# All norms of a two-layer decoder trunk turned unscaled, with the token factor applied where products are read

## The chip, the core and the metric

The kernel runs on one core of a Trainium2 chip. Its metric is the device time of one execution in microseconds. Before the change three runs took 1270.37 to 1271.36 us, with a median of 1271.24. The profile is of a further execution.

A core has TensorE (PE) for matrix products into eight banks of PSUM, VectorE (DVE), ScalarE (ACT) and GpSimd (POOL) for elementwise work, and SyncE (SP), which here only issues transfers. Each engine works through its own instructions in order and waits on semaphores.

## What is computed

A stream x of 256 tokens by 1024 features passes two layers, then a last RMS norm. The reference, cut to what matters:

```python
def rmsnorm(x, w):
    y = x * lax.rsqrt(jnp.mean(x * x, axis=-1, keepdims=True) + NORM_EPS)
    return y * w

memn = rmsnorm(mem, mem_norm_w)
for layer in range(2):
    x = x + 0.5 * swiglu(rmsnorm(x, norm_w[layer, 0]), w_gate[layer, 0], w_up[layer, 0], w_down[layer, 0])
    h = rmsnorm(x, norm_w[layer, 1])
    x = x + (even_mixer(h, ...) if layer % 2 == 0 else odd_mixer(h, ...))
    x = x + cross_attention(rmsnorm(x, norm_w[layer, 2]), memn, wq[layer], wkv[layer], wo[layer])
    x = x + 0.5 * swiglu(rmsnorm(x, norm_w[layer, 3]), w_gate[layer, 1], w_up[layer, 1], w_down[layer, 1])
return rmsnorm(x, final_norm_w)
```

`swiglu(h)` is `(silu(h @ w_gate) * (h @ w_up)) @ w_down` with 2816 hidden features. The even mixer projects h to retention heads (q, k rotated, v, a gate), and to a state-space part: x, B and C go through a causal convolution of four taps and a silu, a step size dt through a softplus with logarithms, and decays between tokens are sums of dt. The odd mixer is sparse and sliding-window attention. The cross attention has four heads over 256 memory tokens, whose keys and values come from `memn`.

A norm has two factors: a weight per feature, and a factor per token, 1/rms (`rstd`). The token factor commutes with a projection: (rstd * x * w) @ W = rstd * ((x * w) @ W).

## The kernel before

**Weights.** All weight matrices stream once through a ring of three slots, in chunks of 1 MB (128 partitions x 2048 floats), on SyncE's queue. `chunk_plan` fixes their order. Each float is split in two parts of lower precision: ScalarE copies `raw` to `w_hi` (`hi_upto`, 1.9 us), VectorE subtracts to `w_lo` (`lo_upto`, 2.3 us), and TensorE adds hi*hi, hi*lo and lo*hi: 48 products of 128x256 or their equal, 5.8 us in a projection and 5.6 in a feed-forward stage. SyncE issues the next load of a slot when VectorE has split it (`lo_done`). `hi_upto(n)` and `lo_upto(n)` make all chunks below n that are not made yet; where such a call stands among other work is written out by hand, engine by engine.

**Stages.** Each layer: a feed-forward stage of 11 turns (gate, up, down chunk), the mixer, the cross attention, a second feed-forward stage. Norms are numbered v: 0 and 5 before the first feed-forward of each layer, 2 and 6 before the mixers, 3 and 7 before the crosses, 4 and 8 before the second feed-forwards, 9 at the end, 1 for the memory.

**Norms.** A projection needs x feature by token (`hT_hi`, `hT_lo`), so TensorE transposes x: 16 transposes of 128x128, as four blocks (t, kh), t for the tokens and kh for half of the features. There are two ways. In the *rows way* (v = 1, 2, 3, 6, 7, 9) ScalarE squares x (`squares`, L614), GpSimd makes `rstd` (L1526, L1528), VectorE scales x to `xn` (`norm_rows`, L1060), TensorE transposes `xn` (L1675), and ScalarE and VectorE split the result from PSUM (`evac_hi` L623, `evac_lo` L1080). In the *column way* (v = 0, 4, 5, 8) TensorE transposes raw x, the weight is applied in the split (`weighted_hi` L632, `weighted_lo` L1070), the squares go beside it, and the token factor is spread over the partitions as a row by a small product (L1769) and applied to gate and up results in the feed-forward stage (L725, L1125). Norm 5 also has two of its blocks transposed between the products of the last down chunk (`turn_ahead`). The memory's norm goes the rows way in the first feed-forward stage, and TensorE transposes it ahead of that stage's last down chunk (`mem_turned`).

**Fillers.** The eight chunks of keys and values of each layer need only the memory. TensorE runs them where it would wait (`FILL` at the norms, `kv_chunk` within the mixers). Chunk (0, 0), the first keys, stands in the even mixer.

**Even mixer.** ScalarE reads each bank of the three convolution chunks x0 to x2 to a padded buffer (L801) and makes the first tap with the bias (L806), VectorE adds six products for the other taps (L1248). ScalarE makes the silus and, for dt, exponentials and logarithms with two table loads. Then VectorE rotates q and k out of PSUM (L1235, four times), GpSimd combines (L1547, L1548) and makes weights for the decay sums (L1572, twice eight), for which TensorE waits at L1935.

## Time and profile before

| | |
|---|---|
| median of three runs | 1271.24 us |
| the profiled execution | 1270.32 us, its span 1268.5 us |
| TensorE products busy | 1243.3 us, 98% |
| VectorE, ScalarE, GpSimd busy | 760.7 us (60%), 624.5 us (49%), 77.5 us (6%) |
| share of the chain that ended last | TensorE 92%, GpSimd 2%, VectorE 2%, ScalarE 2% |
| moved by DMA | 215.29 MB, 170 GB/s in the mean, 284 GB/s in the first of 40 slices |
| mean granted clock of TensorE | 0.990 of full speed |

Idle time of an engine other than TensorE costs nothing by itself. The page gives each group of instructions its busy time and what ended the idle time ahead of it. A single row of the timeline is a run of equal instructions: its start, its length, the engine, the line in the kernel, the operation, output and input tiles, and how many; in brackets the wait ahead of it and the instruction that ended it.

### The profile page before, as it was taken

The numbers are of one execution on the slowest core, as the hardware profiler recorded it, in microseconds if no ns is written. First come the engines' busy times: TensorE is split into PE (matmuls) and PEld (weight loads), VectorE is DVE, ScalarE is ACT, GpSimd is POOL, SyncE is SP. The second block draws the span as 40 slices with busy tenths as digits, with TensorE's granted clock in tenths as the row PEclk, the third lists the DMA queues.
The fourth block names the chain that finished last, engine by engine and source line by source line (L and its number), as shares of the span: only waits on it lengthen the run. The fifth ranks groups of instructions, "written<-read, shape, count | busy, mean of one in ns | idle before, by whom it ended". The sixth has DMA issues, their size and how long they took to land.

```text
span 1268.5 us, 18583 instructions
## 1 busy us (share of the span) xinstructions
PE 1243.3 (98%) x7546; PEld 1098.7 (87%) x7546; DVE 760.7 (60%) x760; ACT 624.5 (49%) x816; POOL 77.5 (6%) x99
## 2 busy tenths in 40 slices
PE   8999998999999999999999999999999999999997
PEld 7888887999989888888898888899877898888886
DVE  6666666754654576665676656645565545756655
ACT  6454445653435464444464444444565345644442
POOL 1000000450110010000010000010000100100000
PEclk9999999999999999999999999999899999999999
DMA  8766663544353455565555655555421434655551
GB/s 284 266 214 199 184 197 117 170 148 148 134 182 133 133 188 187 188 198 183 180 178 188 198 187 179 182 164 180 154 100 34 149 134 133 199 184 181 197 192 40
DMA packets 176931, 215.29 MB, mean 170 GB/s; under 512 B 14768, under 2 KB 159344, under 8 KB 176880
## 3 DMA queue, kind: packets, MB, share of 16 engines
q1 hardware_dynamic: 175792, 211.32, 52.0%
q0 software_dynamic: 864, 3.15, 0.7%
q8 instruction: 37, 0.61, 0.2%
q10 hardware_dynamic: 224, 0.10, 0.0%
q14 instruction: 14, 0.11, 0.0%
HBM read 213.50 MB, written 1.05 MB: 169 GB/s over the span
## 4 chain that ended last, share of the span: by engine, by line
PE 92%; POOL 2%; DVE 2%; ACT 2%; issue 1%; DMA 1%; SPq 0%; DVEq 0%; POOLq 0%; ACTq 0%
PE ps L1620 25%; PE ps L1599 15%; PE ps L1600 15%; PE ps L1601 15%; PE ps L1635 13%; PE ps L1861 1%; PE ps L1675 1%; PE ps L1839 1%; PE ps L2152 1%; POOL xk L1572 1%; ACT w_hi L601 1%; PE ps L2168 1%; ACT ps L614 1%; DVE w_lo L1044 1%; POOL arena L1547 1%
## 5 line engine op out<-in xcount | busy, mean ns | idle before, releaser
L1620 PE MATMUL ps<-hT,w_hi 128*128 128x512 f32 x1392 | 333.3, 392 | 2.2 <-DVE hT L1070 2.2
L1620 PEld LDWEIGHTS ps<-hT,w_hi 128*128 128x128 f32 x1392 | 259.1, 189 | 55.1 <-DVE hT L1070 2.4
L1150 DVE TENSOR_TENSOR w_lo<-raw,w_hi 128x2048 fp32r<-128x2048 f32 x108 | 247.6, 2292 | 62.2 <-ACT w_hi L707 62.2
L1044 DVE TENSOR_TENSOR w_lo<-raw,w_hi 128x2048 fp32r<-128x2048 f32 (+1 forms) x93 | 203.6, 2199 | 125.7 <-ACT w_hi L601 125.5
L707 ACT ACTIVATE w_hi<-raw 128x2048 fp32r<-128x2048 f32 x108 | 206.0, 1908 | 0.0
L601 ACT ACTIVATE w_hi<-raw 128x2048 fp32r<-128x2048 f32 (+1 forms) x92 | 167.8, 1839 | 50.6 <-PE ps L1601 47.1
L1635 PEld LDWEIGHTS ps<-hT,w_lo 128*128 128x128 f32 x1408 | 180.5, 191 | 6.8
L1635 PE MATMUL ps<-hT,w_lo 128*128 128x256 f32 x1408 | 182.6, 283 | 0.0
L1599 PE MATMUL ps<-w_hi,arena_r 128*128 128x512 f32 (+1 forms) x384 | 148.7, 387 | 0.0
L1600 PE MATMUL ps<-w_lo,arena_r 128*128 128x512 f32 (+1 forms) x384 | 148.1, 386 | 0.0
L1601 PE MATMUL ps<-w_hi,arena_r 128*128 128x512 f32 (+1 forms) x384 | 147.8, 385 | 0.0
L1599 PE MATMUL ps<-w_hi,hT 128*128 128x256 f32 (+2 forms) x352 | 113.9, 323 | 0.0
L1600 PE MATMUL ps<-w_lo,hT 128*128 128x256 f32 (+2 forms) x352 | 112.9, 321 | 0.0
L1601 PE MATMUL ps<-w_hi,hT 128*128 128x256 f32 (+2 forms) x352 | 112.9, 321 | 0.0
L1526 POOL TENSOR_SCALAR msq<-msum 128x1 f32<-128x1 f32 x20 | 22.0, 1100 | 1072.2 <-ACT ps L614 659.2
L699 ACT ACTIVATE arena_r<-arena 128x512 fp32r<-128x512 f32 x44 | 27.8, 631 | 119.0 <-PE ps L1601 112.8
L1601 PEld LDWEIGHTS ps<-w_hi,arena_r 128*128 128x128 f32 x384 | 72.1, 188 | 16.1
L680 ACT ACTIVATE arena<-ps 128x512 f32<-128x512 f32 x44 | 26.4, 600 | 118.2 <-PE ps L1635 118.2
L1599 PEld LDWEIGHTS ps<-w_hi,arena_r 128*128 128x128 f32 x384 | 72.3, 188 | 13.9
L1600 PEld LDWEIGHTS ps<-w_lo,arena_r 128*128 128x128 f32 x384 | 72.1, 188 | 13.8
L694 ACT ACTIVATE arena<-ps 128x512 f32<-128x512 f32 x44 | 26.4, 600 | 100.3 <-PE ps L1635 100.3
L1599 PE MATMUL ps<-hT,w_hi 128*128 128x256 f32 x264 | 75.7, 287 | 0.0
(266 smaller groups left out, 1753.5 us busy)
## 6 DMA issues: line engine op xcount, KB each, us to landing
raw<-in_ffn_w_up SPq DMA_DIRECT2D x44, 1024.0 KB, 5.3
raw<-in_ffn_w_down SPq DMA_DIRECT2D x44, 1024.0 KB, 4.8
raw<-in_ffn_w_gate SPq DMA_DIRECT2D x43, 1024.0 KB, 5.3
raw<-in_xattn_wkv SPq DMA_DIRECT2D x16, 1024.0 KB, 5.4
raw<-in_even_w_in SPq DMA_DIRECT2D x13, 1024.0 KB, 5.2
raw<-in_xattn_wq SPq DMA_DIRECT2D x8, 1024.0 KB, 5.1
raw<-in_xattn_wo SPq DMA_DIRECT2D x8, 1024.0 KB, 5.7
raw<-in_even_w_out SPq DMA_DIRECT2D x4, 1024.0 KB, 4.9
```

What stands on the lines that cost most here:

```text
L601: ins = nc.scalar.activation(hi, src, ACT.Copy)
L680: nc.scalar.activation(gate_lo, ps[:, 0:2, SEQ:], ACT.Copy).then_inc(gate_copied, 1)
L694: nc.scalar.activation(up_lo, ps[:, 2:4, SEQ:], ACT.Copy).then_inc(up_copied, 1)
L699: nc.scalar.activation(dst, gu.rearrange("p (k c) -> p k c", k=2), ACT.Copy).then_inc(gu_hi_done, 1)
L707: nc.scalar.activation(w_hi[:, m % RING, :], raw[:, m % RING, :], ACT.Copy).then_inc(hi_done, 1)
L1044: ins = V.tensor_tensor(lo, src, hi.bitcast(F32), ALU.subtract)
L1150: V.tensor_tensor(w_lo[:, m % RING, :], raw[:, m % RING, :], w_hi[:, m % RING, :].bitcast(F32), ALU.subtract).then_inc(lo_done, 1)
L1599: mm(dst, l_hi, r_hi, start=start, stop=False)
L1600: mm(dst, l_hi, r_lo, start=False, stop=False)
L1601: return mm(dst, l_lo, r_hi, start=False, stop=stop)
L1620: mm(ps[:, bank0 + m, :], cols(w_hi, n, k, CW, m * P, (m + 1) * P), hT[:, k, :, :].rearrange("p a c -> p (a c)"), start=k == 0, stop=False)
L1635: last = mm(ps[:, bank0 + m, SEQ:], cols(w_lo, n, k, CW, m * P, (m + 1) * P), hT[:, k, 0, :], start=False, stop=k == KT - 1)
```

## The change

- All norms but the last go the column way, with two blocks transposed inside the last chunk before them (`turn_ahead` before norms 2, 3, 5, 6 and 7). `norm_rows` is left for the last norm alone, and its weight row is loaded late.
- Mixers and crosses take the token factor where their products are read. TensorE spreads it as a row behind the first projection (`rstd_rows`), ScalarE copies the row, and VectorE multiplies with it the results that lie feature by token: the conv chunks (L1270), the queries of the crosses (L1225) and of the odd mixer. These reads were ScalarE's. Results that lie token by feature get it as a scale per partition: on ScalarE in two ACTIVATEs (`tokens_out`), in the rotation on VectorE as a third operand.
- x and the memory are also handed in feature by token (`xT`, `memT`, 1 MB each) and loaded to `turned_raw`. Norm 0 and the memory's norm have no transposes any more: ScalarE and VectorE split `turned_raw` with the weight (`turned_hi`, `turned_lo`), for the memory in turn 7 of the first feed-forward stage. The memory's token factor goes on the keys (VectorE, `k_out`) and values (ScalarE).
- x by token is loaded behind up chunk 0, and ScalarE squares it behind its copy of up chunk 1.
- The key chunk (0, 0) is the filler of norm 2 and has a buffer of its own.
- 13 instead of 10 first products of no use (`WARM`).

```diff
-            take(kv[:7])
+            take(kv[1:7])
...
+        FILL = {("norm", 0, 1): (0, 0), ("norm", 0, 2): (0, 7), ...
...
                 if first:
                     for kh in range(2):
                         ks = slice(4 * kh, 4 * kh + 4)
+                        sp.dma_start(turned_raw[:, ks, :], d["xT"][:, ks, :]).then_inc(xT_in[kh], 16)
                         sp.dma_start(slot_k(base, CW)[:, ks, :], gate[0][:, ks, :])\
...
                 load(base + 1, slot_k(base + 1, CW), up[0])
+                if first:
+                    for t in range(TT):
+                        sp.dma_start(x[:, t, :], d["x"][0, t * P:(t + 1) * P, :]).then_inc(x_in[t], 16)
...
                 hi_upto(base + 4)
-                act.wait_ge(row_mm, f + 1)
-                nc.scalar.activation(rstd_row[:, :], ps[:, 5, 0:SEQ], ACT.Copy).then_inc(row_read, 1)
+                if f == 0:
+                    squares(0, x, lambda t, h: act.wait_ge(x_in[t], 16))
+                row_copy(norm_no(layer, 3 * which), 5)
...
             def even():
                 E = at["even", "x0"]
+                row_copy(2, 7)
                 for c in range(3):
-                    act.wait_ge(chunks_used, E + c + 1)
-                    if c == 0:
-                        act.wait_ge(es["xpad_zero"], 1)
-                    nc.scalar.activation(ev.xpad[:, 2 * c:2 * c + 2, CONV_W - 1:],
-                                         ps[:, c, :].rearrange("p (a c) -> p a c", a=2),
-                                         ACT.Copy)
+                    act.wait_ge(es["xpad_done"], c + 1)
                     for m in range(2):
                         k = 2 * c + m
-                        ins = nc.scalar.activation(ev.xbcT[:, k, :], ps[:, c, m * SEQ:(m + 1) * SEQ], ACT.Identity,
+                        ins = nc.scalar.activation(ev.xbcT[:, k, :], ev.xpad[:, k, CONV_W - 1:], ACT.Identity,
...
+            def k_out(layer, i):
+                dve.wait_ge(chunks_used, at["kv", layer, i] + 1)
+                dve.wait_ge(mem_row_done, 1)
+                V.tensor_tensor(keys(layer, i),
+                                ps[:, KV_BANK[layer][i], :].rearrange("p (a c) -> p a c", a=2),
+                                mem_row[:, :].unsqueeze(1).to_broadcast([P, 2, MEM]), ALU.mult).then_inc(k_read, 1)
...
+                    V.tensor_tensor(ev.xpad[:, 2 * c:2 * c + 2, CONV_W - 1:],
+                                    ps[:, c, :].rearrange("p (a c) -> p a c", a=2),
+                                    rstd_row.unsqueeze(1).to_broadcast([P, 2, SEQ]), ALU.mult)\
+                     .then_inc(es["xpad_done"], 1)
...
+            def rstd_rows(v, bank):
+                pe.wait_ge(rstd_done, 2 * v + 2)
+                rows_of(rstd, bank).then_inc(row_mm, 1)
...
                     turn(j, False)
-                if f == 0:
-                    mem_turned()
...
-                if f == 1:
-                    hidden_down((f + 1) * FJ, n, False, True, turn_ahead(5, ("norm", 1, 0)))
+                if f < 3:
+                    key = ("norm", layer + which, 1 - which)
+                    hidden_down((f + 1) * FJ, n, False, True, turn_ahead(norm_no(key[1], key[2]), key))
...
-                out_chunks(at["mixout", 0, 0], last_bank=lambda: pe.wait_ge(kv_read, 7))
+                out_chunks(at["mixout", 0, 0], last_bank=lambda: pe.wait_ge(*kv_out(0, 6)),
+                           between=turn_ahead(3, ("norm", 0, 2)))
```

ScalarE in the first feed-forward stage, before (the first row is the second half of gate chunk 0, the `w_hi` rows below the squares are up 0, gate 1 and, with `chunks_used`, up 1; the last row copies the factor's row):

```order
L651 ACTIVATE w_hi<-raw 128x1024 [waits raw_in0]
L614 ACTIVATE xn,msum<-x 128x512 [waits x_in0] x2
L614 ACTIVATE xn,msum<-x 128x512 [waits x_in1] x2
L601 ACTIVATE w_hi<-raw 128x2048 [waits raw_in1]
L601 ACTIVATE w_hi<-raw 128x2048 [waits raw_in2]
L680 ACTIVATE arena<-ps 128x512 [waits chunks_used]
L601 ACTIVATE w_hi<-raw 128x2048 [waits chunks_used,raw_in0]
L725 ACTIVATE arena<-ps 128x256 [waits row_mm]
```

And after, with the squares on the lines L627:

```order
L662 ACTIVATE w_hi<-raw 128x1024 [waits raw_in0]
L617 ACTIVATE w_hi<-raw 128x2048 [waits raw_in1]
L617 ACTIVATE w_hi<-raw 128x2048 [waits raw_in2]
L700 ACTIVATE arena<-ps 128x512 [waits chunks_used]
L617 ACTIVATE w_hi<-raw 128x2048 [waits chunks_used,raw_in0]
L627 ACTIVATE arena,msum<-x 128x512 [waits x_in0] x2
L627 ACTIVATE arena,msum<-x 128x512 [waits x_in1] x2
L668 ACTIVATE arena<-ps 128x256 [waits row_mm]
```

The four squares moved from ahead of up 0's copy to behind up 1's, right ahead of the copy of the row for which the factor is needed.

VectorE at the entry of the even mixer, before (`w_lo` rows split weight chunks, L1248 are taps):

```order
L1080 TENSOR_TENSOR hT<-ps,hT 128x4x128 [waits hT_hi_done] x4
L1044 TENSOR_TENSOR w_lo<-raw,w_hi 128x2048 [waits hi_done] x2
L1242 COPY arena<-ps 8x256 [waits e_dt_mm]
L1248 SCALAR_TENSOR_TENSOR arena<-arena,conv_w 128x256 [waits e_act_read]
L1248 SCALAR_TENSOR_TENSOR arena<-arena,conv_w 128x256
L1248 SCALAR_TENSOR_TENSOR arena<-arena,conv_w 128x256 [waits dve_step]
L1248 SCALAR_TENSOR_TENSOR arena<-arena,conv_w 128x256
L1248 SCALAR_TENSOR_TENSOR arena<-arena,conv_w 128x256 [waits dve_step]
L1248 SCALAR_TENSOR_TENSOR arena<-arena,conv_w 128x256
L1044 TENSOR_TENSOR w_lo<-raw,w_hi 128x2048 [waits hi_done]
```

And after (L1088 reads the first keys, L1270 a conv bank, L1278 are taps):

```order
L1045 TENSOR_TENSOR w_lo<-raw,w_hi 128x2048 [waits hi_done]
L1088 TENSOR_TENSOR first_keys<-ps,mem_row 128x512 [waits mem_row_done,chunks_used]
L1045 TENSOR_TENSOR w_lo<-raw,w_hi 128x2048 [waits hi_done] x2
L1265 COPY arena<-ps 8x256 [waits e_dt_mm]
L1270 TENSOR_TENSOR arena<-ps,arena 128x2x256 [waits chunks_used,e_xpad_zero,row_read]
L1278 SCALAR_TENSOR_TENSOR arena<-arena,conv_w 128x256 [waits e_act_read]
L1278 SCALAR_TENSOR_TENSOR arena<-arena,conv_w 128x256
L1278 SCALAR_TENSOR_TENSOR arena<-arena,conv_w 128x256 [waits dve_step]
L1278 SCALAR_TENSOR_TENSOR arena<-arena,conv_w 128x256
L1278 SCALAR_TENSOR_TENSOR arena<-arena,conv_w 128x256 [waits dve_step]
L1278 SCALAR_TENSOR_TENSOR arena<-arena,conv_w 128x256
L1045 TENSOR_TENSOR w_lo<-raw,w_hi 128x2048 [waits hi_done]
```

The read of a conv bank now stands on VectorE ahead of the taps, behind ScalarE's copy of the row, and ScalarE's first tap (`e_act_read`) comes between that read and the other taps.

VectorE at norm 3, before (L1060 scales x, L1080 splits turned x, the `w_lo` rows are key/value chunk 7 and the first query weights):

```order
L1105 SCALAR_TENSOR_TENSOR x<-ps,x 128x512 [waits chunks_used]
L1060 SCALAR_TENSOR_TENSOR xn<-x,rstd,norm_w_rows 128x512 [waits rstd_done,norm_w_in]
L1060 SCALAR_TENSOR_TENSOR xn<-x,rstd,norm_w_rows 128x512
L1044 TENSOR_TENSOR w_lo<-raw,w_hi 128x2048 [waits hi_done]
L1060 SCALAR_TENSOR_TENSOR xn<-x,rstd,norm_w_rows 128x512 [waits rstd_done]
L1060 SCALAR_TENSOR_TENSOR xn<-x,rstd,norm_w_rows 128x512
L1080 TENSOR_TENSOR hT<-ps,hT 128x4x128 [waits hT_hi_done] x4
L1044 TENSOR_TENSOR w_lo<-raw,w_hi 128x2048 [waits hi_done] x4
```

And after (L1066 splits turned x, L1225 reads queries):

```order
L1118 SCALAR_TENSOR_TENSOR x<-ps,x 128x512 [waits chunks_used]
L1066 SCALAR_TENSOR_TENSOR hT<-ps,norm_cols,hT 128x128 [waits cols_hi_done]
L1066 SCALAR_TENSOR_TENSOR hT<-ps,norm_cols,hT 128x128 x3
L1066 SCALAR_TENSOR_TENSOR hT<-ps,norm_cols,hT 128x128 [waits cols_hi_done]
L1066 SCALAR_TENSOR_TENSOR hT<-ps,norm_cols,hT 128x128 x3
L1066 SCALAR_TENSOR_TENSOR hT<-ps,norm_cols,hT 128x128 [waits cols_hi_done]
L1066 SCALAR_TENSOR_TENSOR hT<-ps,norm_cols,hT 128x128 x3
L1045 TENSOR_TENSOR w_lo<-raw,w_hi 128x2048 [waits hi_done] x3
L1225 SCALAR_TENSOR_TENSOR arena<-ps,arena 128x512 [waits chunks_used,row_read]
```

The scaling of x is gone, and all splits of turned x stand ahead of the weight splits, of which one stood between them before.

## Rows read from the trace of the kernel before

**Rows 1.** Waits of TensorE: line <- releaser: total us, times, longest us
```profile
PE ps L1675 <- DVE xn L1060: 7.9, 4, 3.5
PE ps L1620 <- DVE hT L1070: 2.2, 1, 2.2
PE ps L1935 <- POOL xk L1572: 1.2, 1, 1.2
```

**Rows 2.** Timeline of the start: start us, us, engine line op out<-in xcount
```profile
8.12 0.69 DVE L1478 CAST w_hi<-raw 128x1024 fp32r<-128x1024 f32 x1 [8.12 <-DMA raw<-in_ffn_w_gate]
...
12.48 0.75 ACT L614 ACTIVATE xn<-x 128x512 f32<-128x512 f32 x1
...
14.84 0.31 ACT L614 ACTIVATION_READ_ACCUMULATOR xn<-x 128x1 f32 x1
...
16.45 0.57 POOL L1528 TENSOR_TENSOR rstd<-msq,neg_half 128x1 f32<-128x1 f32 x1
...
20.51 1.92 ACT L601 ACTIVATE w_hi<-raw 128x2048 fp32r<-128x2048 f32 x1 [1.27 <-DMA raw<-in_ffn_w_up]
...
21.40 0.68 DVE L1120 TENSOR_TENSOR arena<-arena,ps 128x512 f32<-128x512 f32 x1
...
24.12 3.92 PE L1620 MATMUL ps<-hT,w_hi 128*128 128x512 f32 x16
```

**Rows 3.** Windows of the start; the last three columns: TensorE's clock, DMA share, GB/s
```profile
2.00:4.00 2.00, 2.00 (x11) 2.00 (x11) 0.00 (x0) 1.04 (x1) 0.00 (x0) 1.00 0.84 286
...
12.00:14.00 2.00, 2.00 (x6) 1.51 (x6) 2.00 (x5) 2.00 (x6) 0.00 (x0) 0.50 1.10 348
```

**Rows 4.** Windows at norms 3 and 7
```profile
375.00:380.00 5.00, 4.88 (x27) 4.64 (x28) 3.11 (x6) 1.19 (x2) 0.65 (x1) 0.66 0.85 305
...
1005.00:1010.00 5.00, 2.92 (x24) 2.44 (x23) 4.24 (x5) 1.40 (x3) 3.10 (x3) 1.00 0.23 71
```

**Rows 5.** Timeline, memory's transposes and the entry of norm 2
```profile
191.25 1.91 PE L1675 MATMUL ps<-consts,xn 128*128 128x128 f32 x16
...
198.36 0.40 PE L1601 MATMUL ps<-w_hi,arena_r 128*128 128x512 f32 x1
...
207.39 0.38 PE L1599 MATMUL ps<-hT,small_w_hi 128*128 128x256 f32 x1 [1.41 <-DVE hT L1080]
```

**Rows 6.** Timeline at norm 5
```profile
634.17 0.61 PE L1675 MATMUL ps<-consts,x 128*128 128x128 f32 x4
...
639.31 1.13 DVE L1070 SCALAR_TENSOR_TENSOR hT<-ps,norm_cols,hT 128x128 fp32r<-128x128 f32 x4 [2.12 <-ACT hT L632]
...
640.36 2.29 DVE L1044 TENSOR_TENSOR w_lo<-raw,w_hi 128x2048 fp32r<-128x2048 f32 x1
...
640.80 3.82 PE L1620 MATMUL ps<-hT,w_hi 128*128 128x512 f32 x16
```

**Rows 7.** Timeline of the even mixer
```profile
216.76 1.01 ACT L806 ACTIVATE arena<-ps,conv_b,conv_w 128x256 f32<-128x256 f32 x2
...
217.81 2.71 DVE L1248 SCALAR_TENSOR_TENSOR arena<-arena,conv_w 128x256 f32<-128x256 f32 x6 [5.75 <-ACT arena L806]
...
220.44 2.29 DVE L1044 TENSOR_TENSOR w_lo<-raw,w_hi 128x2048 fp32r<-128x2048 f32 x1
...
238.62 2.44 POOL L1547 TENSOR_TENSOR arena<-arena 128x128 f32<-128x128 f32 x1 [32.86 <-DVE arena L1235]
```

**Rows 8.** Timeline at norms 3 and 7, TensorE
```profile
369.12 0.28 PE L1599 MATMUL ps<-w_hi,memT_hi 128*128 128x256 f32 x1
...
375.11 1.32 PE L1675 MATMUL ps<-consts,xn 128*128 128x128 f32 x8 [2.09 <-DVE xn L1060]
...
380.63 0.28 PE L1599 MATMUL ps<-hT,w_hi 128*128 128x256 f32 x1
...
1003.00 0.28 PE L1599 MATMUL ps<-w_hi,memT_hi 128*128 128x256 f32 x1
...
1013.02 0.28 PE L1599 MATMUL ps<-hT,w_hi 128*128 128x256 f32 x1
```

More of the change, by code:

```diff
@@ L452, in build @@
             pT = part(4096, [XH, 2, SEQ])
-            small = part(6144, [32])
+            small = part(6400, [32])
             nmax = small[:, 0:8]
@@ new lines, in row_copy, with norm @@
+            def row_copy(v, bank):
+                act.wait_ge(row_mm, nth(v) + 1)
+                nc.scalar.activation(rstd_row, ps[:, bank, 0:SEQ], ACT.Copy).then_inc(row_read, 1)
+            def norm(layer, i):
+                v = norm_no(layer, i)
+                weighted_hi(v, SETS["norm", layer, i])
+                squares(v, x, lambda t, h: act.wait_ge(x_added, 4 * (v - 2) + 2 * t + h + 1))
+                if v == 2:
+                    act.wait_ge(mem_row_mm, 1)
+                    nc.scalar.activation(mem_row[:, :], ps[:, 5, 0:MEM], ACT.Copy).then_inc(mem_row_done, 1)
@@ L880, in even, with tokens_out @@
                 kv_chunk(0, 6)
+            def tokens_out(dst, bank, func):
+                for t in range(TT):
+                    ins = nc.scalar.activation(dst[:, t, :], ps[:, bank, t * CW:(t + 1) * CW], func,
+                                               scale=rstd[:, t:t + 1])
+                ins.then_inc(es["act_read"], 1)
             def conv_silu(c):
@@ L1017, in _ @@
             norm(1, 1)
-            hi_upto(at["odd", ODD_ORDER[0]] + 3)
             odd()
-            hi_upto(at["wq", 1, 0])
-            norm(1, 2, ahead=at["wq", 1, 0] + 1)
+            hi_upto(at["wq", 1, 0] + 1)
+            norm(1, 2)
             cross(1)
@@ L1167, in ffn @@
                 lo_upto(base + 4)
-                dve.wait_ge(row_read, f + 1)
+                dve.wait_ge(row_read, nth(norm_no(layer, 3 * which)) + 1)
                 gate_scale(0)
@@ L1364, in odd @@
                         compress_in()
+                lo_upto(at["cmp", 0] + 4)
+                read("qs1", 0)
+                lo_upto(at["odd", "qs1"] + 4)
+                lo_upto(at["cmp", 1] + 4)
+                read("a", 3)
                 lo_upto(at["cmp", 3] + 3)
@@ L1489, in _ @@
             ffn(1, 0)
-            norm(1, 1)
+            lo_upto(at["odd", ODD_ORDER[0]] + 1)
+            k_out(1, 2)
             lo_upto(at["odd", ODD_ORDER[0]] + 3)
             odd()
-            norm(1, 2, ahead=at["wq", 1, 0] + 1)
             lo_upto(at["wq", 1, 0] + 3)
@@ L1667, in used, with transposes @@
                 return ins.then_inc(chunks_used, 1)
-            def transposes(w, ready, src=xn, blocks=None):
-                for t, kh in blocks or block_order(w):
+            def transposes(w, ready, src=xn, blocks=BLOCKS):
+                for t, kh in blocks:
                     ready(t, kh)
@@ L1765, in ffn @@
                 used(wide_lo(base + 1, 2))
[L1767 to L1771 removed]
+                rstd_rows(v, 5)
                 def turn(j, first):
```

468 lines of the change are left out of this document (240 added, 228 removed).

## The prediction

> **What bounds the kernel now.** I read the page first: TensorE is busy 1243.3 of 1268.5 us, and the chain that ended last is TensorE for 92% (both in the table above). So time is won only where TensorE does less, or stands less. Then TensorE's waits by releaser [rows 1]: four waits of its transposes for the scaled x of VectorE (7.9 us together), one for the split of turned x at the start (2.2) and one for GpSimd's segment weights in the even mixer (1.2) are those that the change touches. Last the timeline around each of them, and windows for the granted clock. TensorE's idle time is 25 us in all, 2% of the span; what decides is which of these few microseconds come back elsewhere. The matmuls of the three split products are untouched, and the 16 transposes of each later norm stay, so each part below is a sum over places. 0.2% of the time, about 2.5 us, is what a measurement of this kernel can tell from no change.
>
> **The start.** Before, gate chunk 1 starts at 24.12 [rows 2], right behind the small product that spreads the token factor over the partitions. That product was never late: the last square ended at 15.15 and GpSimd had the factor at 17.02, 1.9 after the squares. In the new order ScalarE squares x behind its copy of up chunk 1, and TensorE keeps the product ahead of gate 1. So gate 1 now hangs on the transfer of up 1. Ahead of that in the queue: x by feature and gate 0 (2 MB), up 0, x by token, gate 1; with up 1 it is 6 MB, 6.3 million bytes. Once it runs, the queue moves 348 GB/s and a little more (I take 355); in its first 2 us it moved 286 [rows 3]. The first half of gate 0, behind 1.57 million bytes in all, released VectorE at 8.12: 2 + 1.57 million / 355 GB/s = 6.4, and 1.7 until it was seen. By the same sum up 1 is seen at 2 + 17.7 + 1.5 = 21.2 (its issue waits for the split of gate 0 at about 13, when the queue is still full, so it isn't late by that). Copy 1.9, four squares 2.7 (12.48 to 15.15), GpSimd 1.9, the product 0.4 [all rows 2]: gate 1 starts at about 27.9, against 24.12. **+3.7.** The first matmul comes earlier, at about 7.8 for 10.94, since no transposes and no split behind them stand ahead; that only makes TensorE ready for gate 1 at about 20.6, and longer waiting. Bounds: +2.5, if the small loads beside the queue take nothing and up 1 is seen 1.2 earlier; +7.5, if 6.3 million bytes go at the rate of the first window.
>
> The clock: after TensorE's wait of 2.09 at 375.11 [rows 8] the granted clock was 0.66 over 5 us [rows 4], so 5 x 0.34 = 1.7 us of matmul time lost. After the wait of the same length in the window from 1005 it stayed at 1.00 (same rows). A wait of 7 us is worse than either; I take the fall. **+1.7.** The Trainium skill ("TensorE: Matmul & The Clock Gate", Part 1) says that an idle TensorE falls to half its 2.4 GHz, and that the moment at which the chip judges is not tied to the kernel, so that the same wait may or may not be followed by a fall. The two rows agree with that, and by it neither new wait is certain to cost its 1.7.
>
> **Memory norm.** Its 16 transposes, 1.91 us between two down products [rows 5], leave TensorE: memory arrives turned. The scalings go to ScalarE and VectorE in turn 7 of the first feed-forward stage, where both have free time in each turn (49% and 60% busy over the span). **-1.9.**
>
> **Entry of norm 2.** Before, from the last down product (198.36, its slot ends 198.59) to the small features at 207.39 [rows 5]: 8.8 us. After, it goes as norm 5 goes now [rows 6]: from the first of the transposes behind the last down chunk, 634.17, around one key chunk to the next stage's first product, 640.80: 6.6 us without a wait. To that come two blocks of transposes moved into the down chunk (0.47 each) and a spread of the memory factor (0.3): 7.9. **-0.9.** And the key chunk, 48 matmuls at 0.12 or 5.8 us, now lies inside and leaves the even mixer: **-5.8.** This is the largest term. It holds only if TensorE doesn't wait where the chunk was taken out, at the mixer's end. There the norm of the mixed heads was 6.4 us ahead of its transposes, and ScalarE's squares of the retention heads move ahead of a copy, which brings it 4 or so forward: slack 4.5 after 5.8 are taken. 0, bounds 0 and +2.
>
> **Even mixer.** Before, ScalarE reads a bank (0.6) and makes the first tap (1.01 for two), VectorE adds six taps (2.71) and splits a weight chunk (2.29) [rows 7]. After, VectorE reads the bank itself, times the factor. No such row exists; the nearest is a product of 128x512 with PSUM, 0.68 (at 21.40) [rows 2]. Per chunk on VectorE: 0.7 + 1.0 in which it stands for ScalarE's tap + 2.7 + 2.3 = 6.7, against TensorE's 5.76 per chunk. The first chunk is late by the spread of the factor and its copy (0.8), and a little by the read that now stands ahead of ScalarE's tap: 1.2. The third by 1.2 + 2 x 0.95 = 3.1. Behind it ScalarE makes the logarithms, VectorE the first rotation, and GpSimd goes on from that (its wait of 32.86, rows 7). Two rotations of eight products, with the factor now 0.26 each as at 639.31 for 0.21, add 1.0. GpSimd's segment weights came 1.2 late already; they are then 4.1 later against TensorE, and the wait of 1.2 becomes about 5.3. **+4.1**, and for the clock as above **+1.7.** The weight splits slip by the same 3 to 4; the one at 220.44 serves the chunk that TensorE starts 5.3 us after its end, so they stay covered. Bounds: 0, if VectorE catches up before the logarithms are there, and +7, if it doesn't until the fourth rotation.
>
> The rows show a bank read of 512 columns at 0.68 on VectorE and the mixer's on ScalarE at 0.60. The Trainium skill ("Perfetto Trace Analysis", Optimizing Scalar/DVE Operations) says that VectorE pays more per instruction for an operand in PSUM than ScalarE does, about 0.07 us; the rows agree. By it, the three reads moved here cost 0.2 more on VectorE than they free on ScalarE.
>
> **Cross and odd entries.** Norm 3 takes from 369.12 to 380.63 [rows 8], 11.5 us, with its wait of 2.1 and the fallen clock. After: two moved blocks 0.95, then as norm 5; but the query projection needs VectorE's split of its first weights, which stands behind the split of turned x: 640.36 + 2.29 - 634.17 = 8.5 [rows 6]. That makes 9.5, with a wait of 2 for the split in the place of the old one. **-1.95.** Norm 7 has the same form and took 1003.00 to 1013.02 [rows 8], without a fall: **-0.5.** Norm 6 took 8.2 with a wait of 0.3 and becomes 0.95 + 6.6: **-0.65.** Four spreads of the factor, for both mixers and both crosses, at 0.3: **+1.2.** The query reads of the crosses go from ScalarE to VectorE, three banks deep: 0, bounds 0 and +1.
>
> **Sum.** 3.7 + 1.7 - 1.9 - 0.9 - 5.8 + 4.1 + 1.7 - 1.95 - 0.5 - 0.65 + 1.2 = +0.7. The profiled run took 1270.32 (its span, 1268.5, and 1.8 around it), so 1271.0; the median of the runs shown is 0.92 above it: **1272.**
>
> **Rivals.** *The clock holds in both new waits.* For it, the window from 1005 [rows 4]; against it, the one from 375. Then -3.4: 1268.6. *VectorE isn't late in the mixer*: before, it stood 1.9 for the logarithms, and it could take part of the lateness there. Against it, the logarithms wait for the third chunk's taps themselves. Then -4.1 - 1.7: 1266.2. *Slower: the start is bound by the transfer rate.* With x in the queue in both layouts, the way to up 1 is 6.3 million bytes, and every microsecond on it falls on gate 1. At the 286 GB/s of the first window [rows 3] they take 22 us instead of 17.7, +4.4: 1276.4. It decides from about 320 GB/s down (+2). Against it, every window from 4 us on shows 348 or more; for it, ScalarE stood for this very chunk before, 1.27 at 20.51 [rows 2], though it was the only one on its way. *The change doesn't do what it says*: the instruction orders show all norms on the new path; no chance of its own.
>
> **Chances.** Forecast 0.42, the clock holds 0.22, VectorE not late 0.13, slow transfers 0.23. The first spans 2.5 to either side and gives 0.34 to no change, 0.05 to faster, 0.03 to slower. The second lies at the bound of 2.5: half and half. So faster 0.29, same 0.45, slower 0.26. The range reaches from the fastest case to the slowest with 1 us more on either side for their own spread: 1265.2 to 1277.5. The likeliest one's own range is 1269.5 to 1274.5.
>
> **What would show it.** At the start TensorE waits for the spread of the factor from about 20.6 to 27.5, with the squares on ScalarE at about 23; wrong if gate 1 starts before 26. In the mixer TensorE waits about 5 us for GpSimd's segment weights, and the first rotation stands about 3 later behind the first projection; wrong if that wait is under 3. At norms 3 and 7 it waits about 2 for the split of the weights. No transposes of memory, and the mixer a chunk shorter. A wait for the mix's end, or for a weight split within the mixer, would make the forecast wrong on the slow side.

## The result, and the profile after

| | before | after |
|---|---|---|
| median, us (8 runs each) | 1270.07 (1269.30 to 1271.36) | 1274.34 (1273.66 to 1275.25) |
| profiled execution: time, span | 1270.32, 1268.5 | 1274.47, 1272.7 |

The ratio is 1.0032, with a 95% interval of 1.0021 to 1.0043. The changed kernel is slower by 4 us, within the recorded range, and outside the 0.2% of no change to which the forecast of 1272.0 had given the largest chance. The sum said +0.7 on the profiled execution; it was +4.2. That 1274.34 lies even within the likeliest case's own range, by 0.2 us, is luck: the base of that range was the median of three runs, 1271.24, and eight runs put it at 1270.07.

From the page of the changed kernel, busy time by engine and the chain that ended last:

```profile
PE 1246.0 (98%) x7539; PEld 1099.6 (86%) x7539; DVE 774.1 (61%) x819; ACT 624.1 (49%) x849; POOL 85.1 (7%) x95
...
PE 92%; DVE 2%; POOL 2%; ACT 2%; DMA 1%; issue 1%; DVEq 0%; POOLq 0%; ACTq 0%
```

TensorE still bounds the kernel, and it is busy 2.7 us longer, though transposes went. The rest is in its waits, listed by releaser (total us, times, longest us):

```profile
PE ps L1760 <- POOL rstd L1580: 6.0, 1, 6.0
PE ps L1987 <- POOL xk L1622: 4.1, 2, 3.2
PE ps L1651 <- DVE w_lo L1045: 3.6, 2, 1.8
PE ps L1672 <- DVE hT L1075: 1.8, 1, 1.8
```

The 7.9 us for the scaled x of [rows 1] are gone. In their place stand the spread of the factor at the start (6.0), the weight splits of norms 3 and 7 (1.8 each), and a wait for GpSimd's segment weights that is 4.1 where it was 1.2. These are the waits that were forecast. The timeline of the start, after:

```profile
18.34 1.91 ACT L617 ACTIVATE w_hi<-raw 128x2048 fp32r<-128x2048 f32 x1 [3.68 <-DMA raw<-in_ffn_w_gate]
...
21.34 1.91 ACT L617 ACTIVATE w_hi<-raw 128x2048 fp32r<-128x2048 f32 x1 [0.60 <-DMA raw<-in_ffn_w_up]
...
23.16 0.61 ACT L627 ACTIVATE arena<-x 128x512 f32<-128x512 f32 x1
...
26.87 0.56 POOL L1580 TENSOR_TENSOR rstd<-msq,neg_half 128x1 f32<-128x1 f32 x1
...
27.49 1.22 PE L1760 MATMUL ps<-consts,rstd 128*128 128x128 f32 x4 [5.98 <-POOL rstd L1580]
28.37 6.13 PE L1672 MATMUL ps<-hT,w_hi 128*128 128x512 f32 x16
```

Up 1 is seen at 21.34 (forecast 21.2), the squares end at about 25.7 and the factor is there at 27.43 (26.87 and 0.56). Gate 1 follows the spread at 28.37, against 24.12 [rows 2]. The windows of the changed kernel (the last three columns are TensorE's clock, DMA share, GB/s):

```profile
28.00:30.00 2.00, 2.00 (x8) 1.71 (x7) 0.83 (x2) 1.23 (x3) 0.00 (x0) 0.50 1.05 363
32.00:34.00 2.00, 2.00 (x8) 1.61 (x7) 0.89 (x2) 1.89 (x2) 0.00 (x0) 0.72 0.00 0
271.00:276.00 5.00, 4.88 (x28) 4.89 (x29) 3.18 (x2) 0.00 (x0) 3.76 (x7) 0.66 0.48 166
380.00:385.00 5.00, 3.18 (x27) 3.01 (x26) 3.35 (x3) 5.00 (x9) 3.65 (x4) 1.00 0.32 100
...
1015.00:1020.00 5.00, 5.00 (x31) 5.00 (x31) 3.88 (x2) 2.89 (x2) 1.16 (x3) 0.66 0.75 222
```

The clock stands at the half level (0.50, which is 1.2 of 2.4 GHz) behind the wait of the start, and is low behind the one in the mixer (271) and the one at norm 7 (1015); behind the equal wait of norm 3 (380) it stays at full. The even mixer of the changed kernel, timeline:

```profile
221.50 0.69 DVE L1270 TENSOR_TENSOR arena<-ps,arena 128x512 f32<-128x512 f32 x1 [1.80 <-ACT arena L668]
...
223.35 2.71 DVE L1278 SCALAR_TENSOR_TENSOR arena<-arena,conv_w 128x256 f32<-128x256 f32 x6 [1.16 <-ACT arena L823]
...
225.98 2.28 DVE L1045 TENSOR_TENSOR w_lo<-raw,w_hi 128x2048 fp32r<-128x2048 f32 x1
...
266.77 1.16 PE L1987 MATMUL ps<-consts,xk 128*128 128x128 f32 x8 [0.95 <-POOL xk L1622]
...
271.12 1.24 PE L1987 MATMUL ps<-consts,xk 128*128 128x128 f32 x8 [3.19 <-POOL xk L1622]
```

VectorE's bank read is 0.69 (forecast 0.7), its stop for ScalarE's tap 1.16 (forecast 1.0), its six products 2.71 and its split 2.28. TensorE waits twice for GpSimd, for the third and the fourth set of segment products.

### The profile page after: what moved, and what is told of

The parts are those of the page before. It is cut to its first block, busy times and chain, and to the rows that moved or that the text cites. A ratio compares the mean times of both kernels' runs of the same rounds, so it can differ in the third digit from the quotient of the medians.

```text
span 1272.7 us, 18668 instructions
## 1 busy us (share of the span) xinstructions
PE 1246.0 (98%) x7539; PEld 1099.6 (86%) x7539; DVE 774.1 (61%) x819; ACT 624.1 (49%) x849; POOL 85.1 (7%) x95
## 3 DMA queue, kind: packets, MB, share of 16 engines
HBM read 212.98 MB, written 1.05 MB: 168 GB/s over the span
## 4 chain that ended last, share of the span: by engine, by line
PE 92%; DVE 2%; POOL 2%; ACT 2%; DMA 1%; issue 1%; DVEq 0%; POOLq 0%; ACTq 0%
PE ps L1672 25%; PE ps L1651 15%; PE ps L1652 15%; PE ps L1653 15%; PE ps L1687 13%; PE ps L1908 1%; PE ps L1886 1%; POOL xk L1622 1%; PE ps L1727 1%; PE ps L2210 1%; DVE w_lo L1045 1%; PE ps L2226 1%; DVE arena L1278 1%; DMA raw<-in_ffn_w_up 1%; POOL arena L1597 1%
## 5 line engine op out<-in xcount | busy, mean ns | idle before, releaser
L1672 PE MATMUL ps<-hT,w_hi 128*128 128x512 f32 x1392 | 336.8, 394 | 2.0 <-DVE hT L1075 1.8
L1578 POOL TENSOR_SCALAR msq<-msum 128x1 f32<-128x1 f32 x20 | 30.8, 1538 | 1096.0 <-ACT xn L627 999.8
```

The costliest lines, as they stand in the source:

```text
L1578: step(G.tensor_scalar(msq[:, t:t + 1], msum[:, 2 * t:2 * t + 1], msum[:, 2 * t + 1:2 * t + 2], EPS, ALU.add, ALU.add))
L1672: mm(ps[:, bank0 + m, :], cols(w_hi, n, k, CW, m * P, (m + 1) * P), hT[:, k, :, :].rearrange("p a c -> p (a c)"), start=k == 0, stop=False)
```

## Where the 4.2 us are

For each place: how much later (or earlier) TensorE stood at the next landmark than before it, after against before, from starts of its instructions in the two timelines.

| place | forecast | measured |
|---|---|---|
| start, to the first down product (35.36 to 41.80) | +5.4 | +6.4 |
| every turn of the four feed-forward stages | none | +2.3 |
| memory's transposes | -1.9 | -1.7 |
| entry of norm 2 | -0.9 | -0.9 |
| key chunk out of the mixer | -5.8 | -5.75 |
| segment weights in the mixer, with the clock | +5.8 | +4.65 |
| norm 3; norm 6; norm 7 | -1.95; -0.65; -0.5 | -2.0; -0.66; -0.47 |
| clock behind norm 7 | 0 | +1.5 |
| clock in the odd mixer (905 to 920) | 0 | -1.05 |
| spreads of the factor | +1.2 | +1.9 |

The measured column sums to +4.2, as the spans differ. The two rows on the clock behind norm 7 and in the odd mixer belong to these two executions and not to the change: in the profile of the arena-alone run below, whose instructions are those of after, the clock held behind norm 7 (1.00 from 1005 to 1020), and its mean from 905 to 925 was 0.74, as before (0.74), where after had 0.83. The largest row that the forecast lacks is the second. It is seen where nothing of the change is at work. Two gate groups of the second feed-forward stage, a turn apart (64 gate and up products and 24 down products in a turn), before:

```profile
510.78 3.79 PE L1620 MATMUL ps<-hT,w_hi 128*128 128x512 f32 x16
...
527.48 3.79 PE L1620 MATMUL ps<-hT,w_hi 128*128 128x512 f32 x16
```

and after:

```profile
513.17 3.83 PE L1672 MATMUL ps<-hT,w_hi 128*128 128x512 f32 x16
...
529.93 3.83 PE L1672 MATMUL ps<-hT,w_hi 128*128 128x512 f32 x16
```

A turn takes 16.70 before and 16.76 after: the same instructions, no wait in either. In the mean of the 36 turns at full clock, the 24 down products take 5.59 us before and 5.615 after, which is 233.0 and 234.0 ns from start to start, and the 16 gate products behind them 3.63 and 3.665. So more than half of the 0.06 falls on the gate products, though they read `hT`, which lies where it lay. Over a stage the longer turn makes 0.54, 0.61, 0.53 and 0.60 us. Two things differ there that an instruction list doesn't show: the changed kernel declares other buffers ahead of the arena, so that `arena_r`, the moving operand of the down products, and the arena itself lie 960 bytes lower in each partition; and the engines beside it work a little differently. The first is easily tried alone.

## The experiments

Each was measured beside the kernel before on one chip. A difference to the changed kernel is (ratio - 1.0032) x 1270 us. By the intervals of the two ratios it is uncertain by about 1.8 us, and by 2 where only five to eight runs were taken. "The clock fell" means that TensorE's clock stood at the half level for a stretch, which cost about 1.5 us behind the waits in the mixer and at norm 7.

**Room ahead of the operand.** The changed kernel with an unused buffer, which puts `arena_r` and the arena at the addresses that they had before:

```diff
         mem_row = sb("mem_row", [P, MEM])
+        sb("room", [P, 240])
```

> The changed kernel with 960 bytes per partition left free ahead of the small weights, so that the working memory (arena_r, arena) lies at the addresses that it has before the change. In the changed kernel a turn of a feed-forward stage takes 16.76 us instead of 16.70, with the same products on TensorE, in all four stages: 44 turns, 2.6 us. Theory A (the addresses of the working memory, against which TensorE reads or the other engines write, set these 0.06 us): the turn is back at 16.70 and the time 2.6 us under the changed kernel's, 1.0011 of before. Rival B (something else, such as the instructions around it or the run): 16.76 stays, and the time is the changed kernel's, 1.0032.

Measured: 1271.65, ratio 1.0013 (1.0004 to 1.0022). Its two gate groups:

```profile
511.80 3.79 PE L1673 MATMUL ps<-hT,w_hi 128*128 128x512 f32 x16
...
528.50 3.79 PE L1673 MATMUL ps<-hT,w_hi 128*128 128x512 f32 x16
```

16.70 again, and 2.4 us of the 4 are gone. Its profiled span is 3.8 shorter than after, 1.5 of which is the clock: behind the wait of norm 7 it stayed at 1.00 here. The turn is thus the firmer evidence of the two.

**The kernel before, moved.** The other way round: the kernel before with one table declared behind the arena instead of ahead of it, so that both stand where the changed kernel has them.

```diff
-        w2 = sb("w2", [P, 2, 2, HD])
+        sb("room", [P, 16])
...
         arena = sb("arena", [P, ARENA])
+        w2 = sb("w2", [P, 2, 2, HD])
```

> The kernel before with one small table moved behind the working memory, so that arena_r and arena lie at the addresses of the changed kernel. Theory A (addresses): turns of 16.76 and 2.6 us more, 1.0020. Rival B: turns of 16.70 and no change, 1.000.

Measured: 1273.56, 1.0021 (1.0012 to 1.0030).

```profile
511.47 3.83 PE L1621 MATMUL ps<-hT,w_hi 128*128 128x512 f32 x16
...
528.23 3.83 PE L1621 MATMUL ps<-hT,w_hi 128*128 128x512 f32 x16
```

16.76, with not one instruction changed. The two together show it: some 2.5 us of the result come from where the buffers lie.

**The arena alone.** The same room, but between the two, so that only the arena returns to its old place and `arena_r` stays in its new one.

```diff
         arena_r = sb("arena_r", [P, 2 * XC_W], F32R)
+        sb("room", [P, 240])
         arena = sb("arena", [P, ARENA])
```

> The changed kernel with the 960 free bytes between arena_r, which TensorE reads, and arena, which only ScalarE and VectorE use in a feed-forward stage, so that arena alone lies where it does before the change. Theory A1 (the place that the other engines use sets TensorE's pace): turns of 16.70 and 2.6 us under the changed kernel. Theory A2 (the place of TensorE's own operand sets it): 16.76 and no change. Products of gate and up do not read arena_r and are 1 ns slower each, which speaks for A1.

Measured: 1274.04, 1.0033 (1.0020 to 1.0045), and the slow turn:

```profile
513.56 3.83 PE L1673 MATMUL ps<-hT,w_hi 128*128 128x512 f32 x16
...
530.32 3.83 PE L1673 MATMUL ps<-hT,w_hi 128*128 128x512 f32 x16
```

So it isn't the arena, which the other engines read and write, but the place of `arena_r`: the moving operand of the down products, which ScalarE and VectorE write. Whether TensorE's reads or their writes are touched was not tried apart.

**The operand aligned.** A room of 104 floats puts `arena_r` at 128 bytes beyond a multiple of 512 in each partition, as the turned x and the weight buffers are. Before it was 160 beyond one, after 224. (No trace shows addresses. The sizes that the kernels declare, each rounded up to 32 bytes, give the distances: against the turned x, `arena_r` is 0, 32 and 96 bytes off.)

```diff
+        sb("room", [P, 104])
```

> The changed kernel with 416 free bytes ahead of the small weights, so that arena_r begins at 128 beyond a multiple of 512 bytes, as hT, w_hi and w_lo do, and not at 224 beyond (changed kernel) or 160 beyond (before). Down products follow each other at 233.9 ns in the changed kernel and at 232.9 before, products of gate and up at 226.7 once they run evenly. Theory (what counts is how arena_r, TensorE's own operand, lies to lines of 64 bytes or more): down products at about 227 too, turns of about 16.56 us, 9 us under the changed kernel, 0.9962. Rival (a down product takes longer for other reasons, and the 1 ns between the two places is all there is): turns of 16.70 to 16.76.

Measured: 1266.70, 0.9973 (0.9962 to 0.9983).

```profile
511.97 3.79 PE L1673 MATMUL ps<-hT,w_hi 128*128 128x512 f32 x16
...
528.55 3.79 PE L1673 MATMUL ps<-hT,w_hi 128*128 128x512 f32 x16
```

A turn of 16.58, the down products 227.8 ns apart, and from the sixth of a group on evenly 226.7. That is 7.5 us less than after, where 9 was expected: the same instructions as after, now faster than before. A multiple of 64 bytes alone can't be all that counts, since 160 and 224 are both 32 beyond one and differ by 1.0 ns a product; whether it is 128, 256 or 512 these three addresses don't tell.

**The squares early.** The start's wait is laid on the squares behind the copy of up 1. Here they stand ahead of the copies of gate 1 and up 1; nothing else moves.

```diff
+                if f == 0:
+                    hi_upto(base + 2)
+                    squares(0, x, lambda t, h: act.wait_ge(x_in[t], 16))
                 hi_upto(base + 3)
                 gate_out(0, base + 1)
                 hi_upto(base + 4)
-                if f == 0:
-                    squares(0, x, lambda t, h: act.wait_ge(x_in[t], 16))
```

> The changed kernel with ScalarE's four squares of x behind the copy of up chunk 0 and ahead of that of gate chunk 1, in the 3.7 us in which ScalarE stands for that chunk's transfer. Theory (the start hangs on the transfer of up chunk 1 through the squares): the token factor is there at about 20.5, the wait of 6.0 at the spread goes, gate chunk 1 starts at about 21.9 instead of 28.4, and the clock stays, 2.2 more: 8.7 us under the changed kernel, 0.9964 of before. Rival (the start is bound by the transfers themselves, so that later chunks wait for what the squares did not): TensorE stands for a copy or split within the next two turns and no more than 3 us come back, 1.001.

Measured: 1267.81, 0.9980 (0.9971 to 0.9989), 6.6 less than after. The mechanism is right and the size too large by 2: the timeline of its start shows a new wait.

```profile
20.36 2.29 DVE L1046 TENSOR_TENSOR w_lo<-raw,w_hi 128x2048 fp32r<-128x2048 f32 x1 [3.34 <-ACT w_hi L617]
...
22.57 0.68 DVE L1131 TENSOR_TENSOR arena<-arena,ps 128x512 f32<-128x512 f32 x1
...
23.31 3.92 PE L1673 MATMUL ps<-hT,w_hi 128*128 128x512 f32 x16 [1.63 <-DVE arena L1131]
```

Gate 1 needs the bank that the sum of gate 0 reads, and on VectorE that sum stands behind the split of gate 1's weights, which had to wait for the copy. The wait for the squares hid it. The first down product comes at 34.55, even earlier than before's 35.36, and the clock doesn't fall behind this wait of 1.63.

**A split between the blocks.** At norms 3 and 7, VectorE splits the first query weights before the last block of turned x instead of behind it.

```diff
-                                        [(0, 0)] if t == 0 else [(0, 1), (1, 0), (1, 1)])
+                                        [(0, 0)] if t == 0 else [(0, 1), (1, 0)])
+                            if t and norm[2] == 2:
+                                lo_upto(last_chunk + 3)
+                            if t:
+                                weighted_lo(norm_no(norm[1], norm[2]), SETS[norm], [(1, 1)])
```

> The changed kernel with the split of the first query weights at norms 3 and 7 between VectorE's splits of turned x, ahead of the last block, for which VectorE stands 2.6 us anyway. Theory (the new wait of 1.8 at each cross is VectorE's order): both waits go, 3.6 us, and with the second the fall of the clock behind it, 1.5: 5.1 us under the changed kernel, 0.9992 of before. Rival (the split only changes places with the last block's, which becomes late by as much): waits of 1 to 2 for the split of turned x, and less than 1 us.

Measured: 1268.68, 0.9992 (0.9983 to 1.0001), 5.1 less than after, as expected. Both waits of 1.8 are gone, and the clock is at 1.00 behind norm 7. How much of the 5.1 is the clock isn't settled, since other profiles held there with the wait in place.

**The segment products apart.** One projection of the even mixer is issued between the second and the third set of segment products.

```diff
                 for q in range(4):
+                    if q == 2:
+                        project(8, ("rot_read", 3))
                     pe.wait_ge(es["ld_done"], 4 * q + 4)
...
-                project(8, ("rot_read", 3))
```

> The changed kernel with TensorE's second value projection of the even mixer between the two halves of the segment products (L1987), instead of behind them. Theory (TensorE stands there 3.2 us for GpSimd's second eight weights, and the clock falls behind it, and no engine behind needs the segment products sooner): the wait of 3.2 goes, that of 0.95 stays, and the clock stays at 1.00: 4.7 us under the changed kernel, 0.9995 of before. Rival (the lateness of VectorE and GpSimd goes on behind the segment products, so that the wait only moves to the transposes of q and k): a wait of 2 or more at those, and 1 to 2 us.

Measured: 1268.27, 0.9988 (0.9979 to 0.9996), 5.6 less than after where 4.7 was expected. TensorE's list of waits has none for the segment weights any more. The excess of 0.9 is within the uncertainty. Luck with the clock doesn't make it in the profile: the clock held behind norm 7, where it had fallen after, but fell behind norm 3 (0.66 from 376 to 381), where it had held.

**The factor left out.** To price the factor's part in VectorE's lateness, the three conv chunks are read without the token factor (that part of the computation is left out), by ScalarE as before.

```diff
-                    act.wait_ge(es["xpad_done"], c + 1)
+                    act.wait_ge(chunks_used, E + c + 1)
+                    nc.scalar.activation(ev.xpad[:, 2 * c:2 * c + 2, CONV_W - 1:], ps[:, c, :]..., ACT.Copy)
...
-                    V.tensor_tensor(ev.xpad[:, 2 * c:2 * c + 2, CONV_W - 1:], ps[:, c, :]..., ALU.mult)
```

> The changed kernel with ScalarE reading the three convolution banks as before the change; the token factor of these three chunks is left out. Theory (the read on VectorE and its standing for ScalarE's tap make the first rotation 2.85 us late): the rotation starts 26.5 us behind the first projection instead of 29.4, the waits at the segment products fall from 4.1 to 1.3 together, and the clock stays, 1.5: 4.3 us under the changed kernel, 0.9998 of before. Rival (the rotations with the factor and GpSimd set it): the waits stay above 3, and less than 1.5 us.

Measured: 1269.63, 0.9996 (0.9987 to 1.0004), 4.6 less than after. One wait for the segment weights is left, and it is longer than expected:

```profile
PE ps L1987 <- POOL xk L1622: 2.0, 1, 2.0
```

The factor's part is 2.1 of the 4.1 us of waiting. The expectation that the clock would stay is wrong: it fell for as long as after, only earlier, with the kernel (0.66 from 268 to 273). The profiled execution took 1273.05, 3.4 above the median of its runs, so it doesn't show where the other 2.5 of the 4.6 us are. What is left of the wait above the 1.2 of before would fit the rotation with a third operand, which this kernel keeps (2.15 us for eight products, 1.67 before); that wasn't tried.

**The split in the gap.** VectorE splits the weights while it stands for ScalarE's tap, instead of behind its products.

```diff
                      .then_inc(es["xpad_done"], 1)
+                    lo_upto(E + c + 3)
                     dve.wait_ge(es["act_read"], c + 1)
...
-                    lo_upto(E + c + 4)
+                    if c == 2:
+                        lo_upto(E + c + 4)
```

> The changed kernel with VectorE's weight split of one chunk earlier in the 1.16 us in which it stands for ScalarE's tap in the second and third convolution chunk. Theory (VectorE's 6.9 us per chunk are more than TensorE's 5.76, and only the third chunk's end counts): the third chunk's taps end 1.0 earlier, the waits at the segment products are 3.1 instead of 4.1, 1.0 us under the changed kernel, 1.0024 of before. Rival (the split in the gap is longer than the gap and delays the taps): 1 us more.

Measured: 1272.35, 1.0020 (1.0012 to 1.0029), 1.5 less than after, where 1.0 was expected: by the times alone that isn't clear of the uncertainty. Its waits show it, since only the second of the two is left:

```profile
PE ps L1989 <- POOL xk L1624: 3.2, 1, 3.2
```

Together the two waits went from 4.1 to 3.2, as expected. The third and the fourth set both need weights of GpSimd's second pass,

```profile
264.38 6.68 POOL L1622 TENSOR_SCALAR xk<-consts,arena 128x128 f32<-128x128 f32 x8
```

(timeline of the changed kernel, eight weights in 6.7 us), and between these two sets TensorE has nothing else to do. So an earlier rotation first takes away the wait of 0.95, and then shortens the other one: with the factor left out the pass ends earlier still, and the wait was 2.0.

**The keys back.** The largest term of the forecast, tried alone: the first key chunk returns from the entry of norm 2 to the even mixer.

```diff
-            take(kv[:1])
             take([("even", x) for x in EVEN_ORDER])
-            take(kv[1:7])
+            take(kv[:7])
...
-        FILL = {("norm", 0, 1): (0, 0), ("norm", 0, 2): (0, 7), ...
+        FILL = {("norm", 0, 2): (0, 7), ...
```

> The changed kernel with the first key chunk back in the even mixer, so that norm 2 has no filler. Theory (the chunk covers a wait that is there without it, and its whole 5.8 us leave the mixer): from the last down product to the small features about 4 us instead of 7.1, with a wait of about 3 for the split of turned x, and the mixer 5.8 longer: 2.6 us over the changed kernel, 1.0053 of before. Rival (the mixer's end stood on TensorE's chunks, and with one more of them nothing else changes, but the wait at norm 2 brings the clock down): 4.3 us over, 1.0066. Second rival (the chunk taken out of the mixer uncovered a wait there, as at the segment products): less than 1 us over.

Measured: 1277.88, 1.0060 (1.0047 to 1.0074), 3.6 more than after, where 2.6 was expected. Its entry of norm 2:

```profile
204.97 0.64 PE L1729 MATMUL ps<-consts,x 128*128 128x128 f32 x4
...
209.17 0.36 PE L1653 MATMUL ps<-hT,small_w_hi 128*128 128x256 f32 x1 [2.09 <-DVE hT L1069]
```

4.2 us from the third block of transposes to the small features, with TensorE idle for 2.1 of them and 0.4 more before the last block, where after has 7.1 with a chunk of 5.8 inside. The mixer is 5.9 longer. So at the entry the chunk costs 2.9, since it fills 2.5 us of waiting, and in the mixer 5.9, which places 3.0 us. The spans of the two profiles differ by 3.8: 0.2 more is ahead of the entry, and the clock in the odd mixer was lower here (0.74 from 905 to 925, for 0.83), which is the execution's luck. The clock stayed at 1.00 from 205 to 210.

**All together.** The room of 240, the early squares (with the sum of gate 0 ahead of the split of gate 1, which the squares experiment asked for), the split between the blocks, the segment products apart and the split in the gap. The last two lines are what is new in it:

```diff
+                if f == 0:
+                    lo_upto(base + 2)
+                    gate_sum(0)
                 lo_upto(base + 3)
-                gate_sum(0)
+                if f:
+                    gate_sum(0)
```

> The changed kernel with all that helped: arena_r and arena at their addresses of before, the squares of x early, and with them ScalarE's and VectorE's read of gate 0 ahead of gate 1's copy and split (it was the wait of 1.6 that took the place of the old one), the split of query weights between the blocks, the segment products in two halves, the split in the gap. Theory (the parts add up: 2.6, 7.3 + 1.6, 5.1, 5.6): about 22 us under the changed kernel, 0.986 of before, and no wait over 1.5 us behind the start. Rival (the next chain is close behind at the start or in the mixer): a wait of 2 or more in one of the two, 0.990.

Measured: 1251.08, 0.9851 (0.9838 to 0.9865), 23 less than after, where 22 was expected. And the same with the room of 104, which aligns the operand:

```diff
-        sb("room", [P, 240])
+        sb("room", [P, 104])
```

> The kernel of all that helped, with arena_r at 128 beyond a multiple of 512 bytes. Theory as for that place alone: 6 us under the same kernel with the addresses of before, 0.981. Rival: the same time as that one.

Measured: 1245.64, 0.9808 (0.9794 to 0.9821), 5.4 less than without the alignment, where 6 was expected, and 24 us faster than the kernel before. From its page, and its timeline where the wait of the start was (the last row is cut by the window, it shows 12 of gate 1's 16 products):

```profile
PE 1230.5 (99%) x7539; PEld 1093.1 (88%) x7539; DVE 775.0 (62%) x819; ACT 624.3 (50%) x849; POOL 83.3 (7%) x95
```

```profile
17.65 0.69 DVE L1139 TENSOR_TENSOR arena<-arena,ps 128x512 f32<-128x512 f32 x1 [0.65 <-ACT arena L701]
...
20.96 0.60 PE L1775 MATMUL ps<-consts,rstd 128*128 128x128 f32 x4
21.32 3.01 PE L1687 MATMUL ps<-hT,w_hi 128*128 128x512 f32 x12
```

Gate 1 starts at 21.32 without a wait, since the sum is done at 18.3, and the longest wait of TensorE in the whole kernel is 1.5. The same 7539 matmuls keep it busy 1230.5 us for 1246.0, because it runs at full clock nearly everywhere (mean 0.997, after 0.989) and the down products stand closer. A fall in the odd mixer is left (0.54 from 890 to 895).

## Why the prediction came out as it did

**Start, +5.4 forecast, +6.4 measured.** The order of events was right. The first matmul came 0.4 later than forecast (8.19 for 7.8) and TensorE was ready for gate 1 0.9 later (21.5 for 20.6), which cost nothing, since the factor came later still. On the path that counted, up 1 was 0.14 late, the four squares took 2.5 for 2.7, GpSimd had the factor 1.7 us behind them (forecast 1.9), and the spread itself ran at half clock and held gate 1 back for 0.9 instead of 0.4. The start is thus +4.25 for +3.7, and the clock 2.2 for 1.7: gate 1's group of 16 takes 6.13 against 3.92 [rows 2]. The price of a fall had been read off behind a wait of 2 us [rows 4]; behind one of 6 the windows from 28 to 34 show it lasting longer. The rival of slow transfers didn't happen: from 4 to 22 us the queue moved 348 to 404 GB/s. The argument against that rival rested on a misread row, though: in the kernel before, the windows show 348 or more only from 4 to 14 us, and 61 and 202 in the two behind.

**Memory, entry of norm 2, key chunk: right.** -1.7, -0.9 and -5.75. At the mixer's end TensorE doesn't wait, so the slack that had been worked out was there. The keys experiment confirms the term from the other side, with 5.9.

**Mixer, +5.8 forecast, +4.65 measured.** VectorE per chunk, the tap's gap and the rotation (2.85 later behind the first projection, forecast 3.1) were as worked out. But the wait that was forecast at 5.3 was 4.1, in two parts: GpSimd's second pass ended 3.6 later behind the first projection, not 4.1, and the spread of the factor made TensorE itself 0.4 later, which the forecast hadn't taken off. The clock cost 1.5, where 1.7 was forecast. Without the factor on the conv chunks half of the waiting goes, and with a projection moved between the sets all of it. The rival *VectorE isn't late* is wrong.

**Norms: right in the waits, wrong in one clock.** The waits for the split came, 1.82 and 1.81 for the forecast 2, at

```profile
382.36 0.35 PE L1651 MATMUL ps<-hT,w_hi 128*128 128x256 f32 x1 [1.82 <-DVE w_lo L1045]
...
1014.63 0.35 PE L1651 MATMUL ps<-hT,w_hi 128*128 128x256 f32 x1 [1.81 <-DVE w_lo L1045]
```

and with the split moved between the blocks they go. Behind the second the clock fell (+1.5), behind the first it didn't; the forecast had no fall at either, which was a chance of its own and had no case in it. Against that the odd mixer's fall of clock, which both kernels have, was 1.05 us cheaper. Both are luck of the profiled execution: the arena-alone run, with the same instructions, had them the other way (held behind norm 7, and in the odd mixer as long a fall as before).

**Spreads, +1.2 forecast, +1.9 measured.** Each costs 0.43 to 0.5, not 0.3. The price was that of four small products alone; what the rest is wasn't tried.

**The step that failed** is one that the forecast didn't have. Its opening says that the matmuls of the split products "are untouched, and the 16 transposes of each later norm stay, so each part below is a sum over places". The instructions are untouched, but their operand isn't where it was: `arena_r` moved by 960 bytes, the 24 down products of a turn became 0.02 us slower and the 16 gate products behind them 0.03, and over all turns that is +2.3 us, the larger half of the 3.5 that the sum missed. So the term was put at nothing without a look at where the buffers lie. The rest is the start (+1.0), the clock of norm 7 (+1.5) and the spreads (+0.7), less the mixer (-1.15) and the odd mixer's clock (-1.05). Without the failed step the kernel would have come out at about +1.9, within 0.2%; the room of 240 gives 1.0013.

## What to carry to other kernels

When a change declares or resizes a buffer, look where the operands of the busiest engine come to lie, before and after, and time the new code once with the old addresses; a turn of a loop that the change doesn't touch is the place to see it. Where a producer is late, first try to put other work of the waiting engine ahead of its wait: one projection moved took away both waits and won 5.6 us here, while the earlier producer took 0.9 off waits of 4.1. And when a long wait goes, the next one behind it in the same chain was hidden by it (gate 1's, 1.63 here), so list all that the waiting instruction needs, not only what came last.

## What the runs showed of the hardware

- The place of the moving operand of fp32r products (128x128 weights, 512 columns) goes with their spacing: 227.8 ns at 128 beyond a multiple of 512 bytes, 233.0 at 160, 234.0 at 224. Over the kernel that is 7.5 us between the last and the first. The distance of their starts shows it best: by their mean durations they take 391 ns at the first place and 395 to 397 at the others, so the step from 160 to 224 is hardly seen there. The first gate products behind them are slower too at 224, though their own operand didn't move. The mechanism stays open.
- Equal waits don't bring equal clocks. Behind 2.09 us at norm 3 of the kernel before it fell to 0.66, behind as long a wait at norm 7 it held at 1.00 [rows 4]; with its buffers moved and no instruction changed, it fell at both. Nine profiles have the changed kernel's waits of 1.8 at norms 3 and 7: behind norm 3 the clock fell in three of them, behind norm 7 in four, and in none behind both. The Trainium skill ("TensorE: Matmul & The Clock Gate", Part 1) says that the moment at which the chip judges isn't tied to the kernel; these runs agree. So a single profile carries about 1.5 us of luck for each such wait. The last two kernels have neither these waits nor a fall at these places.
